# Eighteen pairs of value tiles a layer as seven block products instead of thirteen, their token differences moved to GpSimd, and gates split two tiles per operation

## The reference, cut to what matters

```python
def peer_ffn(x, w_q, subkeys, u, v):
    ...
    idx = jnp.take_along_axis(cidx, pos, axis=-1).reshape(PEER_CHUNK, PEER_HEADS * PEER_TOPK)
    gate = jax.nn.softmax(top, axis=-1).reshape(PEER_CHUNK, PEER_HEADS * PEER_TOPK)
    u_e = jnp.take(u, idx, axis=0)
    v_e = jnp.take(v, idx, axis=0)
    act = jax.nn.gelu(jnp.einsum('ted,td->te', u_e, xc).astype(jnp.float32))
    return jnp.einsum('te,ted->td', (gate * act).astype(v_e.dtype), v_e)
```

## Time and profile before

| what | value |
|---|---|
| median of three runs | 2605.15 us (2605.06 to 2608.98) |
| profiled execution: its time, its span | 2605.46 us, 2603.6 us |
| granted TensorE clock over the span | 0.999 |
| v stage of layer 0, first to last matmul start | 657.4 to about 997 us of the span |
| v stage of layer 1 | 1582.0 to about 1921 us |
| busy over the span | PE 2569.0 us (99%), DVE 2046.8 (79%), ACT 1419.9 (55%), POOL 707.6 (27%) |

### The profile page before, as it was taken

The page is one execution under the profiler, slowest core; times in us unless marked ns, Lnnn a source line. Parts: engine busy times, 40 slices in busy tenths (PEclk is TensorE's granted clock), DMA queues, the critical chain, the costliest instruction groups (busy, mean ns, idle before and its releaser), DMA issues.

```text
span 2603.6 us, 39192 instructions
## 1 busy us (share of the span) xinstructions
PE 2569.0 (99%) x14507; PEld 2205.1 (85%) x14507; DVE 2046.8 (79%) x3506; ACT 1419.9 (55%) x2177; POOL 707.6 (27%) x354
## 2 busy tenths in 40 slices
PE   9999999999999999999999999999999999999998
PEld 8888888888888887788888888888888888998887
DVE  6566799888788887877998887888888667756884
ACT  4343667444565664645775445666654457543543
POOL 0001788777000002015887772000010021100000
PEclk9999999999999999999999999999999999999999
DMA  6455455444655555344554446565545555213554
GB/s 246 162 174 186 166 187 187 161 155 159 209 198 201 199 198 188 113 154 163 190 191 162 155 160 214 201 202 197 205 156 187 193 171 172 73 66 114 186 189 160
DMA packets 125133, 452.34 MB, mean 174 GB/s; under 512 B 13952, under 2 KB 14080, under 8 KB 124944
## 3 DMA queue, kind: packets, MB, share of 16 engines
q1 hardware_dynamic: 122976, 442.62, 50.5%
q0 software_dynamic: 1968, 7.22, 0.9%
HBM read 447.68 MB, written 2.10 MB: 173 GB/s over the span
## 4 chain that ended last, share of the span: by engine, by line
PE 93%; DVE 4%; ACT 1%; issue 1%; POOL 0%; DMA 0%; DVEq 0%; SPq 0%; POOLq 0%; ACTq 0%
PE ps L689 26%; PE ps L686 14%; PE ps L719 10%; PE ps L721 10%; PE ps L720 10%; PE ps L706 2%; PE ps L708 2%; PE ps L707 2%; PE ps L840 2%; DVE W L1857 2%; PE ps L880 2%; PE ps L881 2%; PE ps L879 2%; PE ps L1028 1%; PE ps L663 1%
## 5 line engine op out<-in xcount | busy, mean ns | idle before, releaser
L1329 ACT ACTIVATE hi<-ring 128x1024 fp32r<-128x1024 f32 (+1 forms) x829 | 856.0, 1038 | 202.1 <-PE ps L721 104.9
L2862 POOL TENSOR_TENSOR ring_r<-ring,hi 128x1024 fp32r<-128x1024 f32 x260 | 621.7, 2406 | 1151.2 <-ACT hi L1329 1150.9
L1890 DVE TENSOR_TENSOR ring_r<-ring,hi 128x1024 fp32r<-128x1024 f32 (+1 forms) x569 | 680.7, 1202 | 176.0 <-ACT hi L1329 172.0
L689 PE MATMUL ps<-xT_r,hi 128*128 128x512 f32 x2944 | 719.3, 393 | 0.0
L689 PEld LDWEIGHTS ps<-xT_r,hi 128*128 128x128 f32 x2944 | 536.3, 188 | 100.6 <-DVE W L1857 0.2
L686 PE MATMUL ps<-xT_r,ring_r 128*128 128x256 f32 x2944 | 395.7, 284 | 0.0
L686 PEld LDWEIGHTS ps<-xT_r,ring_r 128*128 128x128 f32 x2944 | 380.8, 191 | 14.4
L719 PE MATMUL ps<-hi,oht_r 128*128 128x512 f32 x832 | 324.0, 389 | 0.3 <-DVE oht_r L1857 0.2
L720 PE MATMUL ps<-ring_r,oht_r 128*128 128x512 f32 x832 | 323.8, 389 | 0.0
L721 PE MATMUL ps<-hi,oht_r 128*128 128x512 f32 x832 | 323.8, 389 | 0.0
L1439 ACT ACTIVATE spare<-ps 128x256 f32<-128x256 f32 x256 | 98.2, 384 | 268.5 <-PE ps L689 145.6
(11 more groups left out here) (353 smaller groups left out, 3621.1 us busy)
## 6 DMA issues: line engine op xcount, KB each, us to landing
ring<-in_peer_u SPq DMA_DIRECT2D x256, 512.0 KB, 3.2
ring<-in_peer_v SPq DMA_DIRECT2D x256, 512.0 KB, 3.4
ring<-in_f SPq DMA_DIRECT2D x132, 512.0 KB, 4.3
ring<-in_ret_vg SPq DMA_DIRECT2D x32, 512.0 KB, 3.3
ring<-in_peer_q SPq DMA_DIRECT2D x32, 512.0 KB, 3.5
ring<-in_ret_out SPq DMA_DIRECT2D x16, 512.0 KB, 3.3
ring<-in_ret_qk SPq DMA_DIRECT2D x15, 512.0 KB, 3.3
ring<-in_in_shift SPq DMA_DIRECT2D x14, 512.0 KB, 3.8
```

What stands on the lines that cost most here:

```text
L689: ins = pe.matmul(b, hi[n][:, c], xT[:, k, :], start=not turn and k == 0, stop=k == 7, skip_group_check=True)
L1329: hid.done(a.activation(hi[m % NH][:, 0:n], ring[j % NR][:, 0:n], ACT.Copy), j)
L1890: lo_v.done(v.tensor_tensor(low_part[j % NR][:, 0:n], ring[j % NR][:, 0:n], as32(hi[m % NH][:, 0:n]), ALU.subtract), j)
L2862: lo_p.done(p.tensor_tensor(low_part[j % NR][:, :], ring[j % NR][:, :], as32(hi[m % NH][:, :]), ALU.subtract), j)
```

## The change

`PAIRS` becomes k = 12, 18, ..., 114, eighteen pairs a layer. The four `differences` of DVE become three operations on GpSimd (two of them merged into one of 256 columns), which wait for the pair before to be done with `V_x`. `prep` handles two tiles per operation, in even passes only, on ACT and DVE; it fills two slots at once, so that in pass k it waits until tile k-1 (of the pair before, where it is one) is multiplied, where it was tile k-2 before. `V_sum_hi`, `V_x_hi` and `V_x_low` swap places in `W`.

```diff
@@ -40,7 +40,8 @@
 TILE_US = 2.77
 JOIN_LEAD = -2.0
 GATE_SCALE = 2.0 ** 14
-PAIRS = tuple(range(18, 115, 8))
+PAIR_STEP = 6
+PAIRS = tuple(range(12, 115, PAIR_STEP))
@@ -308,8 +309,8 @@
         P_equal, P_hot = [[ohh[:, o + q * 2048:o + q * 2048 + 1024].rearrange("p (j z n s) -> p j z n s", j=2, z=2, s=2)
                            for q in range(2)] for o in (0, 1024)]
         P_prep = ohr[:, :].rearrange("p (s t) -> p s t", s=4)
-        V_sum, V_sum_low, V_sum_hi = xTt[:, 2048:4096], xTr[:, 2048:4096], WF[:, 0:2048]
-        V_x_hi, V_x_low, V_x = WF[:, 2048:2560], WF[:, 2560:3072], spare[:, 0:512]
+        V_sum, V_sum_low, V_sum_hi = xTt[:, 2048:4096], xTr[:, 2048:4096], WF[:, 1024:3072]
+        V_x_hi, V_x_low, V_x = WF[:, 0:512], WF[:, 512:1024], spare[:, 0:512]
@@ -1443,11 +1444,11 @@
                         a.wait_ge(*at(dve, "gated", l, 63))
                     if k == 126:
                         a.wait_ge(*at(dve, "gelu", l, 126))
-                    if k - 5 in PAIRS:
-                        a.wait_ge(*at(mm, "pair", l, k - 5))
+                    if k - 4 in PAIRS:
+                        a.wait_ge(*at(mm, "pair", l, k - 4))
                     elif k >= 4:
-                        a.wait_ge(*at(mm, "eaten", TILE["peer_v", l * 128 + k - 4]))
-                    act.done(a.activation(P_prep[:, k % 4, 0:256], Wv[:, k, :], ACT.Copy), "prep", l, k)
+                        a.wait_ge(*at(mm, "eaten", TILE["peer_v", l * 128 + k - 3]))
+                    act.done(a.activation(P_prep[:, k % 4:k % 4 + 2, 0:256], Wv[:, k:k + 2, :], ACT.Copy), "prep", l, k)
                 exps = {EXP_TILE[tt]: tt for tt in range(2)}
                 for i in range(128):
@@ -1468,15 +1469,14 @@
                         act.done(a.activation(W[:, t * 256:t * 256 + 1024].rearrange("p (n i) -> p n i", n=8), b3(iota, [128, 8, 128], 1),
                                               ACT.Identity, bias=1.0, scale=0.0), "ones", l)
                 prep(0)
-                prep(1)
                 low_half(127)
                 gelu(126)
                 def pair_x(k):
-                    a.wait_ge(*at(dve, "pair_diff", l, k))
+                    a.wait_ge(*at(pool, "pair_diff", l, k))
                     if k > PAIRS[0]:
-                        a.wait_ge(*at(mm, "pair", l, k - 8))
+                        a.wait_ge(*at(mm, "pair", l, k - PAIR_STEP))
                     act.done(a.activation(V_x_hi, V_x, ACT.Copy), "pair_x", l, k)
                 def pair_sum(k, n):
@@ -1486,7 +1486,7 @@
                     act.done(a.activation(V_sum_hi[:, t], V_sum[:, t], ACT.Copy), "pair_sum", l, k)
                 for k in range(128):
-                    if k < 126:
+                    if k < 126 and k % 2 == 0:
                         prep(k + 2)
                     split(TILE["peer_v", l * 128 + k] + 2)
                     if k + 4 in PAIRS:
@@ -2208,8 +2208,9 @@
                 def prep(k):
                     v.wait_ge(*at(act, "prep", l, k))
-                    hi_part = P_prep[:, k % 4, :]
-                    dve.done(v.tensor_tensor(hi_part[:, 256:512], Wv[:, k, :], as32(hi_part[:, 0:256]), ALU.subtract), "prep", l, k)
+                    two = P_prep[:, k % 4:k % 4 + 2, :]
+                    dve.done(v.tensor_tensor(two[:, :, 256:512], Wv[:, k:k + 2, :], as32(two[:, :, 0:256]), ALU.subtract), "prep", l, k)
+                    dve.also("prep", l, k + 1)
                 def gated(g):
@@ -2251,7 +2251,7 @@
                     u1, u3, u2, u4 = (V_sum[:, j * 512:j * 512 + 512] for j in range(4))
                     if n == 0:
                         if k > PAIRS[0]:
-                            v.wait_ge(*at(mm, "pair", l, k - 8))
+                            v.wait_ge(*at(mm, "pair", l, k - PAIR_STEP))
                         v.wait_ge(*arrived(ta))
                         v.wait_ge(*arrived(tb))
                         dve.done(v.tensor_tensor(u1, wa[:, 0:512], wa[:, 512:1024], ALU.add))
@@ -2259,17 +2259,6 @@
                     else:
                         tt_(u2, u1, wb[:, 512:1024], ALU.add)
                         tt_(u4, u2, wb[:, 0:512], ALU.add, name=("sum", l, k, 1))
-
-                def differences(k):
-
-                    x4 = W[:, k * 256:k * 256 + 512]
-                    s3, s1, s2, s4 = (V_x[:, j * 128:j * 128 + 128] for j in range(4))
-                    if k > PAIRS[0]:
-                        v.wait_ge(*at(act, "pair_x", l, k - 8))
-                    step(v.tensor_tensor, s3, x4[:, 0:128], x4[:, 128:256], ALU.subtract)
-                    dve.done(v.tensor_tensor(s1, x4[:, 384:512], x4[:, 128:256], ALU.subtract))
-                    tt_(s2, s1, x4[:, 0:128], ALU.add)
-                    tt_(s4, x4[:, 256:384], s2, ALU.subtract, name=("pair_diff", l, k))
                 def low_x(k):
@@ -2311,13 +2300,11 @@
                 for k in range(127):
                     if k + 2 in PAIRS:
                         sums(k + 2, 1)
-                    if k < 126:
+                    if k < 126 and k % 2 == 0:
                         prep(k + 2)
                     split(TILE["peer_v", l * 128 + k] + 2)
                     if k in (4, 6, 8, 10, 12):
                         next(whole, None)
-                    if k + 5 in PAIRS:
-                        differences(k + 5)
                     if k + 4 in PAIRS:
                         low_x(k + 4)
                     if k + 3 in PAIRS:
@@ -2899,6 +2886,24 @@
                 for i in range(128):
                     split(TILE["peer_u", l * 128 + i] + 2)
                 gains(l, 0, mm, "peer_u", l, 127)
+
+                def differences(k):
+
+                    x4 = W[:, k * 256:k * 256 + 512]
+                    s1, s2, s4 = (V_x[:, j * 128:j * 128 + 128] for j in range(1, 4))
+                    if k > PAIRS[0]:
+                        p.wait_ge(*at(dve, "pair_x", l, k - PAIR_STEP))
+                    p.wait_ge(*(at(act, "pair_x", l, k - PAIR_STEP) if k > PAIRS[0] else at(dve, "prep", l, 4)))
+                    x3 = x4.rearrange("p (j n) -> p j n", j=4)[:, 0:4:3, :]
+                    pool.done(p.tensor_tensor(V_x[:, 0:256].rearrange("p (j n) -> p j n", j=2), x3, b3(x4[:, 128:256], [128, 2, 128], 1),
+                                              ALU.subtract))
+                    p.wait_ge(pool.sem, pool.n)
+                    pool.done(p.tensor_tensor(s2, s1, x4[:, 0:128], ALU.add))
+                    p.wait_ge(pool.sem, pool.n)
+                    pool.done(p.tensor_tensor(s4, x4[:, 256:384], s2, ALU.subtract), "pair_diff", l, k)
+
+                for k in PAIRS:
+                    differences(k)
                 if l:
                     gains(l, 1, dve, "natural", l, 0)
                 split(TILE["peer_v", l * 128 + 127] + 1)
```

## The result

| | before | after |
|---|---|---|
| median, seven runs each | 2605.86 us (2605.06 to 2608.98) | 2615.44 us (2614.28 to 2616.13) |
| profiled execution: time, span | 2605.46, 2603.6 | 2616.13, 2614.3 |
| v stage of layer 0, of layer 1 | 340.31, 340.73 | 343.74, 344.10 |
| from the end of the one to the start of the other | 584.22 | 588.68 |

After over before is 1.0033 (95%: 1.0023 to 1.0043): the change made the kernel 0.37% slower by the medians. The single times of the kernel before fall in two groups, about 2605 and 2608.5; the profiles compared here are of the lower group unless the text says otherwise. A v stage is counted from its first matmul to the first transpose (L522, now L523) of the stage behind it.

The account below looks back on a forecast made before the run. The prediction took TensorE (PE), busy for 99% of the span, as the bound. Matmuls -6.8, steady pairs +7.5 and first pairs +5.0 gave +5.7 us, so 2610.8 against the median, 0.22% slower, range 2601 to 2622.

Parts of the forecast that it names:

- matmuls: v stages: ten more pairs, three matmuls less each, 30 x 0.2267 = -6.8 us, hidden by nothing.
- steady pairs: v stages: GpSimd blocks DVE by 0.9, so PE waits 0.22 for `low_sums` at each of 34 pairs, +7.5 us.
- first pairs: First pair of each layer: `x` operations in its chain and GpSimd make PE wait 2.5 us, +5.0 in all.
- last three tiles: End of each v stage: not priced apart; lone tiles' low parts were held to be ready in time, at no cost.
- The step that failed: Chain to `low_sums`: pairs at six tiles instead of eight leave DVE 0.68 us a pair before PE waits.
- What costs nothing: v stages: two-tile `prep` waiting one tile longer, `prep` at the stage's start, and the burst of loads cost nothing.
- the prediction's own last paragraph: Signs in the changed profile: PE idle before each pair's tenth matmul; wrong as a whole if PE waits elsewhere.
- Rival 1: v stages: slack covers GpSimd's blocking, only first pairs stall, -3.6 to -1.8 us, 2601.5 to 2603.3; chance 0.25.
- Rival 2: v stages: not even the first pair stalls, -6.8 to -5.2 us, 2598.4 to 2600; chance 0.10.
- Rival 3: v stages: GpSimd operations block DVE for their whole length, 1.63 a pair, +31.9 us, 2637; chance of +12 or more 0.22.
- Rival 4: v stages: the burst of loads lands over 2 us later than priced and each pair waits for DMA; chance 0.03.

Follow-up runs that it names:

- the last run: Changed kernel with differences back on DVE, norm operations in passes 3 to 6, `prep` of tiles 126 and 127 single, picks through PSUM: 2598.78 us, 0.9974.
- The rewrite: Changed kernel, last top-k operations in the u stages write scaled gates as picks and into PSUM, no SBUF-to-SBUF copy: 2611.77 us, 1.0025.
- the memsets: Changed kernel with two GpSimd memsets of 256 columns a pair ahead of the differences: 2615.69 us, 1.0035.

## Why the prediction was right, and where not

The forecast was 2610.8 with a range of 2601 to 2622, slower the likeliest; 2615.44 lies in it. The direction was right, and the v stages came out near their sum (+6.8, +5.7 forecast). But 6.1 of the 10.7 us between the two profiles lie in two places that the forecast put at nothing; it is the width of the range that covers them, and not the mechanism. The parts of the sum, in us over both layers:

| term | forecast | measured |
|---|---|---|
| matmuls | -6.8 | -6.8 (layer 0 of the last run: -3.35 a layer) |
| steady pairs | +7.5 (34 x 0.22) | +6.7 (32 x 0.21) |
| first pairs | +5.0 | +5.0 (2 x 2.48) |
| last three tiles | 0 | +1.6 |
| both v stages | +5.7 | +6.8 |
| between them | 0 | +4.5 |

The terms of the v stages add up to 6.5; 0.3 of their 6.8 is not placed. The spans differ by 10.7: 6.8 + 4.5, less 0.3 by which the first v stage began earlier and 0.3 behind the second.

1. *The steady pairs.* The size was right in every link: DVE blocked for 0.96 (0.9 forecast), `low_sums` at 10.65 behind the pair's end (9.49 + 1.15 = 10.64 forecast), PE late by 0.21 (0.22). 16 pairs a layer stall and not 17: the last has no differences behind it to block its sums. One price was misread without effect: `low_sums` is 2.28 long, but 2.21 from its start to the next start (725.30 to 727.51), and the chain needs its length.
2. *The step that failed* is where the slack was said to come from: "The distance between pairs shrinks from eight tiles to six", and "Before the change the same distance was two tiles longer, and PE did not wait". Thirteen pairs, eight tiles apart, stalled by the same 0.21; eighteen with one-tile `prep` did not stall. What used up the slack is two-tile `prep`, and it takes both to stall a steady pair: two-tile `prep` with the differences on DVE did not stall either. Two-tile `prep` was costed as a saving and, in "What costs nothing", as one tile of waiting that nobody feels. That it ties the split of tile K-2 to the end of tile K-5 (for one-tile `prep` K-6, which in a pair is done after three matmuls) was in the chain as its starting point, not as an effect of the change. That the number came out right all the same was luck: at six tiles both readings begin at the same matmul.
3. *The first pair.* 2.48 measured, 2.5 forecast, and 1.53 without GpSimd (differences on DVE, layer 0), where 1.6 was forecast; moving the norm operations took off 2.28 and left the steady 0.21. Only the place was wrong. All of the wait was put in front of the tenth matmul, but more than half of it came in front of the fourth, where PE needs the split of the pair's second tile. The forecast's own chain has that split start at 10.87, or 11.77 with GpSimd's 0.9, when PE is at that matmul by 4 x 2.72 + 3 x 0.23 = 11.57; `low_sums` stands right behind the split, so the total did not change.
4. *The last three tiles.* The sentence "a lone tile's low part is then ready 3.0 us after PE starts the tile two before it, which takes 5.4" leaves out that the last three tiles are taken by quarters, so that tile 127 is wanted one quarter after tile 126. Cost 0.8 a layer. By the prediction's own last paragraph a wait of PE in front of a lone tile meant that it was wrong as a whole; this is such a wait, though the chain of the pairs stood beside it.
5. *Layer 1's u stage.* No step named it. Where the same instructions of the two traces are compared, 0.5 of the 4.5 lies ahead of the picks, 2.1 at them, and 1.9 behind. The 2.1 is the wait, which goes with the blocked cast. The 1.9 fits the window behind it: 10 us at 0.83 are 1.7 us lost. Ahead of that window PE had stood still for the wait of 1.97. In the run with the norm operations earlier PE waited 2.00 too and the clock stayed at 1.00; it has 0.5, 2.2 and 0.3 in the three places, and the run with differences on DVE is like it (0.4, 2.2, 0.3). So the wait alone does not always bring the lower clock. The rewrite, which took the wait away, took 4.25 with it.
6. *The rivals.* Rival 1's regime, in which slack covers the blocking, is what one-tile `prep` gives. Rival 2, the clean gain, was reached with all four losses gone (2598.78). One-tile `prep` alone comes close to it: its v stages are 6.2 shorter together than before, and three of its seven times lie at 2598.0 to 2598.7. Rival 3 is refuted: the three operations, 1.63 long by its prices, cost 0.96, and the 256 columns more, 0.73 long, cost 0.54 at their sum and 0.42 a pair. Rival 4 did not occur in the changed kernel.

What stays open is the upper group of times of the kernel before. It did not go with the cast. One run points at the clock: with `prep` of one tile the profiled execution was in its upper group, and its window between 2328 and 2336 us, in a later stage that no edit touches, reads

```profile
2328.00:2336.00 8.00, 8.00 (x33) 6.95 (x32) 3.69 (x10) 0.38 (x1) 1.02 (x1) 0.57 0.01 2
```

A granted clock of 0.57 over 8 us loses 3.4 us, near the distance between that kernel's groups (2598.0 to 2598.7 and 2601.0 to 2601.8). PE had waited 0.77 for DVE two microseconds earlier; it waits 0.8 at the same place in the kernel before, profiled in its lower group, and the clock there stayed at 1.00. There is no trace of the kernel before in its upper group. The granted clocks on record point the same way: beside the experiments it ran 37 times in the upper group, each time at 0.998, and of its 53 times in the lower group 47 were at 0.999 or 1.000. What lowers the clock in one execution and not in the next stays open.

## What to carry to other kernels

Merging two operations into one also merges their waits: ask what the first half may now no longer do early, and put that in the sum beside the instructions saved. Work moved to GpSimd was free here in three cases: where it read nothing from SBUF (the memsets), where the DVE operation beside it took one operand from SBUF and one from PSUM (the rewritten picks; the cast from SBUF to SBUF was blocked, though it has one operand), and where the chain behind DVE had slack (one-tile `prep`). Find that slack by the event that starts the chain, not by the distance between its ends. A stage that ends in another order than it runs (here the last three tiles by quarters) needs its own check.

## What was not expected of the hardware

- A DVE operation with one SBUF and one PSUM operand took 0.29 for 128 columns while GpSimd splits ran; the cast from SBUF to SBUF, 0.23 to 0.27 when free, took 2.23 to 2.26 when a split of 2.4 was ahead of it.
- Two engines that start within 0.01 us of each other gave two stable patterns in one execution, six pairs of 5.45 and then only 4.76.
- GpSimd operations of one length cost DVE different amounts: one of 128 columns cost 0.26 at the second sum and 0.14 or 0.15 at the third and fourth. So an extra read of 256 columns, 0.54 at its own sum, came to only 0.42 a pair.
